# First value units on the un-normed residual, scaled afterwards, in a one-core hybrid decoder step

## What is computed

```
xn = x * rsqrt(mean(x*x) + eps) * norm_mix
lru_x, lru_g, q, k, v = split(xn @ w_in)
y_lru = (recurrence(conv(lru_x)) * gelu(lru_g)) @ w_branch_lru
q, k = rmsnorm(q, q_gain), rmsnorm(k, k_gain)         # per head
y_att = merge(three dilated window groups of q, k, v) @ w_branch_att
g_lru, g_att = sigmoid(xn @ w_merge + b_merge)
x = x + (g_lru*y_lru + g_att*y_att) @ w_o
x = x + (silu(gate) * up) @ w_ffn_out                 # gate, up = rmsnorm(x) @ w_ffn_in
```

## Time and profile before

| | us |
|---|---|
| median of 3 runs | 2105.46 |
| lowest, highest | 2101.01, 2105.50 |
| profiled execution, its own time | 2102.43 |
| its span, first to last instruction | 2100.6 |
| TensorE busy in it | 2023.8 |
| VectorE, ScalarE, GpSimd busy | 927.7, 510.1, 552.2 |

### The profile page before, as it was taken

The page is one execution under the profiler, slowest core; times in us unless marked ns, Lnnn a source line. Parts: engine busy times, 40 slices in busy tenths (PEclk is TensorE's granted clock), DMA queues, the critical chain, the costliest instruction groups (busy, mean ns, idle before and its releaser), DMA issues.

```text
span 2100.6 us, 33178 instructions
## 1 busy us (share of the span) xinstructions
PE 2023.8 (96%) x12884; PEld 1952.6 (93%) x12884; DVE 927.7 (44%) x1222; ACT 510.1 (24%) x791; POOL 552.2 (26%) x331
## 2 busy tenths in 40 slices
PE   5799999999989999999989989999999999999999
PEld 4799889999989999999988889999999999999999
DVE  8466667777714333333256563433321324202331
ACT  5466643333314433333311011210100000000000
POOL 2233322322221111111121142322323323323232
PEclk9899999999999999999999999999999999999999
DMA  3111112222252332333467353111111111111112
GB/s 128 44 43 42 42 45 80 84 96 80 90 196 86 130 126 91 126 126 112 134 229 262 121 192 140 47 45 50 41 50 50 40 50 50 40 50 46 44 53 87
DMA packets 71592, 188.39 MB, mean 90 GB/s; under 512 B 9313, under 2 KB 28796, under 8 KB 70780
## 3 DMA queue, kind: packets, MB, share of 16 engines
q1 hardware_dynamic: 41456, 136.97, 19.3%
q10 hardware_dynamic: 30092, 50.81, 6.6%
HBM read 145.09 MB, written 45.81 MB: 91 GB/s over the span
## 4 chain that ended last, share of the span: by engine, by line
PE 90%; DVE 4%; DMA 3%; issue 2%; ACT 1%; POOL 0%; SPq 0%; ACTq 0%; DVEq 0%; POOLq 0%
PE ups L485 66%; PE ups L585 13%; PE ups L610 3%; PE aux L634 3%; PE aux L509 1%; PE aux L536 1%; PE aux L622 1%; PE ups L622 1%; DMA bt_s<-u_s 1%; DVE ext L1169 1%; DMA o_s<-x 1%; DVE x L1430 0%; DMA x<-x_T 0%; DVE ext L1165 0%; DMA x<-o_s 0%
## 5 line engine op out<-in xcount | busy, mean ns | idle before, releaser
L485 PE MATMUL ups<-big,wsp 128*128 128x344 f32 x9360 | 1508.3, 322 | 18.4 <-POOL wsp L454 6.6
L485 PEld LDWEIGHTS ups<-big,wsp 128*128 128x128 f32 x9360 | 1485.7, 189 | 39.6 <-issue 26.6
L452 POOL CAST wsp<-wraw 128x1024 fp32r<-128x1024 f32 (+2 forms) x160 | 165.5, 1035 | 1494.2 <-issue 698.1
L454 POOL TENSOR_TENSOR wsp<-wraw,wsp 128x1024 fp32r<-128x1024 f32 (+2 forms) x160 | 380.7, 2380 | 12.8
L585 PE MATMUL ups<-big,wsp 128*128 128x344 f32 x1728 | 302.9, 326 | 1.6 <-ACTq L968 1.6
L585 PEld LDWEIGHTS ups<-big,wsp 128*128 128x128 f32 x1728 | 271.3, 189 | 7.1 <-issue 5.2
L1265 DVE RECIPROCAL x<-x 128x1024 f32<-128x1024 f32 x24 | 157.3, 6553 | 75.3 <-ACT x L931 75.3
L1323 DVE SCALAR_TENSOR_TENSOR x<-ups,ext 128x128 f32<-128x128 f32 (+1 forms) x192 | 58.3, 345 | 215.1 <-PE ups L610 126.2
L1128 ACT ACTIVATE ext<-ext 128x1032 f32<-128x1032 f32 x22 | 23.5, 1068 | 482.5 <-DVE ext L1529 482.4
L1531 DVE TENSOR_TENSOR ext<-ups,ext 128x1032 f32<-128x1032 f32 x22 | 27.1, 1233 | 215.4 <-PE ups L485 215.4
L1545 DVE TENSOR_TENSOR x<-ups,x 128x1032 f32 x24 | 29.6, 1233 | 203.6 <-PE ups L485 203.6
(11 more groups left out here) (187 smaller groups left out, 1114.4 us busy)
## 6 DMA issues: line engine op xcount, KB each, us to landing
...
```

Of the source, the lines that this page charges most:

```text
L452: nc.gpsimd.tensor_copy(hi, raw).then_inc(w_hi, 1)
L454: nc.gpsimd.tensor_tensor(lo, raw, hi.bitcast(F32), ALU.subtract).then_inc(w_split[slot], 1)
L485: ins = nc.tensor.matmul(ups[:, slot, c, 0:CH], wsp[:, slot, w, k, :], src[:, a, k, c * CH:(c + 1) * CH], start=(k == 0 and w + a == 0), s ...
```

## The change

The two pairs `v` move from behind the queries to the very start of `stream`. The first value pair doesn't take the normed input: ScalarE multiplies each residual tile by `norm_mix` as it lands (the high part, in `big2`), VectorE makes the low part (L1224), and TensorE multiplies it tile by tile, the second unit two tiles behind the first (`LEAD`). Squares are added by VectorE and GpSimd beside that, and the ones-products (`first_sums`) are put among the last tiles. The second value pair takes the same un-normed input. ScalarE copies the outputs (`values_out`), VectorE scales them by the reciprocal root (`values_scaled`) and then makes the normed input in place in the residual's buffers (`normed`, `normed_low`), which is first used by the first recurrence pair.

That pair runs as two whole units, with its gate products behind them. The last two gate chunks of the recurrence are put between the chunks of the first query unit. The bias lines are made before everything else. The first attention pair follows the last key unit at once, with a tile table of its own (`FIRST_PIECES`), the last head statistics inside it and the bias tile loaded behind them; query and key tiles, value tiles and others change their buffers so that they can be loaded earlier. The square sum of the decode rows goes to the stage `ylru`.

```diff
+        x_sq = big1_f32[:, 0]
+        sums, odd_sums, rinv = x_sq[:, 0, :], x_sq[:, 1, :], ext[:, 0, 0:NT]
...
+            ("v", 2, KT, A["w_in"], 40, 41, 2, 0),
             ("lru", 8, KT, A["w_in"], 0, 8, 1, 0),
             ("qk", 12, KT, A["w_in"], 16, 17, 2, 0),
-            ("v", 2, KT, A["w_in"], 40, 41, 2, 0),
...
-        QT, KTT, VT = tmp(0)[:, 0:SEQ], tmp(1)[:, 0:SEQ], tmp(2)[:, 0:SEQ]
+        QT, KTT, VT = ext[:, 2, 0:SEQ], ext[:, 3, 0:SEQ], tmp(2)[:, 0:SEQ]
...
+        FIRST_PIECES = (16, 24, 28, 31, 34, 37, 40, 42, 44, 46, 48)
...
-            for k in range(KT):
-                sp.dma_start(tmp(k), A["x_T"][k]).then_inc(x_loaded[k], 16)
...
+                if name == "v":
+                    first = 1
+                    weights(0, 0)
+                    for k in range(KT):
+                        sp.dma_start(tmp(k), A["x_T"][k]).then_inc(x_loaded[k], 16)
+                        if k == 1:
+                            weights(0, 1)
+                    for dst, con in consts:
+                        sp.dma_start(dst, con).then_inc(const_ld, 16)
...
-                        sp.wait_ge(qn_stored[j], 16 * 13)
-                        sp.wait_ge(v_stored[j], 16)
-                    sp.wait_ge(sq_normed, 1)
+                        sp.wait_ge(v_stored[j], 16 * 2)
+                    sp.wait_ge(qn_stored[0], 16 * 8)
+                    query_loads(0, 0)
+                    sp.wait_ge(qsl_done[0], 12)
                     value_load(0, 0)
                     sp.wait_ge(bt_fill, 16)
-                    query_loads(0, 0)
-                if name == "lru":
-                    first = 1
-                    weights(0, 0)
-                    weights(0, 1)
-                    for dst, con in consts:
-                        sp.dma_start(dst, con).then_inc(const_ld, 16)
+                    sp.wait_ge(st_done[1], 13)
+                    bias_load(0, 0)
...
+                    pool.wait_ge(nsq_done, 5)
+                    nc.gpsimd.tensor_tensor(odd_sums, odd_sums, x_sq[:, 4, :], ALU.add).then_inc(odd_done, 1)
+                    pool.wait_ge(nsq_done, 8)
+                    pool.wait_ge(odd_done, 1)
+                    nc.gpsimd.tensor_tensor(odd_sums, odd_sums, x_sq[:, 7, :], ALU.add).then_inc(odd_done, 1)
+                    split(name, nk, 1, 0)
+                    split(name, nk, 1, 1)
+                    low(POOL_LOW[0])
+                    continue
+                if name == "lru":
+                    first = 1
+                    split(name, nk, 0, 0)
+                    low(POOL_LOW[1])
+                    low(POOL_LOW[2])
+                    split(name, nk, 0, 1)
...
+            pe.wait_ge(lines_ld, 48)
+            bias_line(0)
+            bias_line(1).then_inc(u_ps, 1)
+            pe.wait_ge(u_sb, 1)
+            bias_line(2).then_inc(u_ps, 1)
...
+            LEAD = 2
+            for n in range(KT + LEAD):
+                if n < KT:
+                    if n == 0:
+                        pe.wait_ge(w_split[0], T0["v"] + 2)
+                        pe.wait_ge(ps_free[0], T0["v"] + 1)
+                    pe.wait_ge(xlo_done, n + 1)
+                    raw_tile(0, n)
+                if n == 7:
+                    pe.wait_ge(u_sb, 2)
+                    pe.wait_ge(ones_done, 1)
+                    pe.wait_ge(sum_done, 1)
+                    first_sums(0)
+                    first_sums(1)
+                if n == 8:
+                    pe.wait_ge(nrt_done, 1)
+                    first_sums(2)
+                if n >= LEAD:
+                    if n == LEAD:
+                        pe.wait_ge(w_split[1], T0["v"] + 2)
+                        pe.wait_ge(ps_free[1], T0["v"] + 1)
+                    raw_tile(1, n - LEAD)
+            unit("v", 1, 0, big2)
+            unit("v", 1, 1, big2)
...
+            unit("lru", 0, 0, big1, ready=normed_ready)
+            unit("lru", 0, 1, big1)
+            gates(0, 0)
+            with pe.Fori(1, KT) as i:
                 for c in range(NCH):
-                    unit("lru", i, 0, big1, parts=(c,), ready=partial(wait_split, pe, 0) if first else None)
-                    if first:
-                        unit("lru", i, 1, big1, parts=(c,))
-                    elif c < 2:
+                    unit("lru", i, 0, big1, parts=(c,))
...
-            gates(KT - 1, 1)
-            gates(KT - 1, 2)
-            pe.wait_ge(gate_ev, KT * NCH + 1)
...
+                    if first and j == 0:
+                        for c in range(2):
+                            unit("qk", i, j, big1, parts=(c,))
+                            gates(KT - 1, c + 1)
+                        pe.wait_ge(gate_ev, KT * NCH + 1)
+                    else:
+                        unit("qk", i, j, big1, parts=(0, 1))
...
-            unit("v", 0, 0, big1, parts=(0, 1))
-            stats(1, 11)
-            unit("v", 0, 0, big1, parts=(2,))
-            pe.wait_ge(rt_done[1], 13)
-            pe.wait_ge(lines_ld, 48)
-            bias_line(0)
-            bias_line(1).then_inc(u_ps, 1)
-            unit("v", 0, 1, big1)
-            pe.wait_ge(u_sb, 1)
-            bias_line(2).then_inc(u_ps, 1)
-            pe.wait_ge(sm_dve, 1)
-            nc.tensor.matmul(aux[:, 1, 0:192], bones[:], sqs, start=True, stop=True).then_inc(sm_pe, 1)
-            unit("v", 1, 0, big1)
-            unit("v", 1, 1, big1)
...
-                    if g == 0:
+                    if first:
+                        stats(1, 11)
+                        pieces(8, marks[0])
                         pe.wait_ge(ps_free[1], T0["att0"] + 1)
-                        pe.wait_ge(u_sb, 2)
-                        pe.wait_ge(sm_act, 1)
+                        pe.wait_ge(rt_done[1], 13)
...
+                if g == 0:
+                    pair(0, True, FIRST_PIECES)
+                with pe.Fori(int(g == 0), 4) as i:
+                    pair(i, False, PIECES)
...
-            y_chunks(0, 3)
+            y_chunks(0, 1)
+            head_squares()
+            y_chunks(1, 3)
...
+            act.dma_start(gmix[:], A["c_norm_mix"]).then_inc(gmix_ld, 16)
+            act.dma_start(lines.rearrange("p (g n) -> p g n", g=NG), A["c_lines"].rearrange("g b n -> b g n")).then_inc(lines_ld, 16)
+            act.dma_start(relx[0:NBK, :], A["rel_bias"]).then_inc(lines_ld, 16)
+            act.dma_start(relx[NBK:NBK + 1, :], A["c_one"]).then_inc(lines_ld, 16)
+            act.wait_ge(gmix_ld, 16)
             for k in range(KT):
-                square(0, k, k % 2)
+                act.wait_ge(x_loaded[k], 16)
+                nc.scalar.activation(big2[:, 0, k, :], tmp(k), ACT.Identity, scale=gmix[:, k:k + 1]).then_inc(xhi_done, 1)
+                nc.scalar.activation(x_sq[:, k, :], tmp(k), ACT.Square).then_inc(nsq_done, 1)
+                if k == 2:
+                    act.wait_ge(u_sb, 2)
...
+            values_out(0)
+            values_out(1)
+            values_store(0)
+            values_store(1)
+            for k in range(4):
+                normed_hi(k)
+            values_out(2)
+            for k in range(4, KT):
+                normed_hi(k)
+            values_store(2)
...
+            values_out(3)
+            values_store(3)
...
+            act.wait_ge(sm_pe, 1)
+            nc.scalar.activation(rms, aux[:, 1, 0:192], ACT.Sqrt, scale=1.0 / HD, bias=epst[:]).then_inc(sm_act, 1)
...
+            dve.wait_ge(u_ps, 1)
+            nc.vector.tensor_copy(u_lines[:, 0:2, :], aux[0:HG, :, 0:UL]).then_inc(u_sb, 1)
+            dve.wait_ge(u_ps, 2)
+            nc.vector.tensor_copy(u_lines[:, 2, :], aux[0:HG, 0, 0:UL]).then_inc(u_sb, 1)
             for k in range(KT):
-                norm_add(k, 0, k % 2)
+                dve.wait_ge(xhi_done, k + 1)
+                nc.vector.scalar_tensor_tensor(big2[:, 1, k, :], tmp(k), gmix[:, k:k + 1], big2[:, 0, k, :].bitcast(F32),
+                                               ALU.mult, ALU.subtract).then_inc(xlo_done, 1)
+                if k > 1 and k not in POOL_LOW:
+                    dve.wait_ge(nsq_done, k + 1)
+                    step.step(nc.vector.tensor_tensor(sums, sums, x_sq[:, k, :], ALU.add))
+            dve.wait_ge(odd_done, 2)
+            nc.vector.tensor_tensor(sums, sums, odd_sums, ALU.add).then_inc(sum_done, 1)
+            for c in range(NCH):
+                dve.wait_ge(nrt_done, c + 1)
+                step.step(nc.vector.reciprocal(part(rinv, c), part(rinv, c)))
+
+            def values_scaled(n):
+                j = n % 2
+                dve.wait_ge(ps_free[j], n // 2 + (T0["v"] + 2))
+                nc.vector.tensor_tensor(VO[j], VO[j], rinv, ALU.mult).then_inc(vm_done, 1)
+
+            def normed(k):
+                nc.vector.scalar_tensor_tensor(tmp(k), tmp(k), gmix[:, k:k + 1], rinv, ALU.mult, ALU.mult).then_inc(nf_done, 1)
+
+            def normed_low(k):
+                if k not in POOL_LOW:
+                    dve.wait_ge(nhi_done, k + 1)
```

(17 more changed lines are left out.)

240 lines of the change are left out of this document (101 added, 139 removed).

## The result

The changed kernel takes 2087.81 us (median of 4 runs, 2086.37 to 2091.51), the kernel before 2104.51 in the same comparison (4 runs): a ratio of 0.9923, 95% interval 0.9906 to 0.9940. A repeat on another chip gave 2085.91 (5 runs) against 2103.62, 0.9921 (0.9908 to 0.9935). Forecast was 2078 with a range of 2066 to 2090 and 0.95 on faster. Direction and range held, but by the profiled executions the gain is 16.1 us (2102.43 to 2086.37) where the sum said 25.7.

A forecast was written before the change was run, and what follows sets the result against it. TensorE was busy 2023.8 of 2100.6 us, leaving some 77 us idle and a little low clock. Terms 15.6 + 3.5 - 45.8 + 1.0 = -25.7 took 2102.43 to 2076.7, as a median 2078, range 2066 to 2090.

The forecast's parts named there:

- (a) to (c): Start up to the first value pair and sums: first low part done at 13.0 us, this stretch ending at 39.6.
- (d): Second value pair beside VectorE's norming, to 62.2 us: last low part ready about 62.5, wanted 65.5; cover 3, charged 2.
- (B): Rival: port collisions of VectorE and GpSimd in the start come out in full, about +7 us, giving 2085; chance 17%.
- the rule from the Trainium skill: VectorE instructions with two SBUF inputs contend with GpSimd instructions reading SBUF; passes take 3.24 us against 1.23.
- The mark set for (B): Profile sign at the first recurrence gates: forecast near 87 us; a start later than 92 means (B) holds.
- The end of the recurrence: Last gates moved into the first query unit: gain 0.3 us, cold restart +2.8, GpSimd's weight split +1.0; sum +3.5.
- (A): Rival: no wait at the first query statistics, since the chain behind the last gate shortens; up to -12 us, 2067; 8%.
- From the last key unit to attention: Hand-over into attention: scores start 43.5 us earlier, idle gaps of 2.7 and 4.5 us; sum -45.8.
- E: End of the last unit before attention, about 563.4 us; scores start at E + 60.4 before, E + 16.9 after.
- The decode rows: Square sum and root moved into the next stage, nearly all hidden by VectorE's idle time: 0 to 3 us, taken as 1.
- The sum: Whole kernel: 15.6 + 3.5 - 45.8 + 1.0 = -25.7 us, from the profiled 2102.43 to 2076.7.
- (C): Rival: every two-input VectorE pass of the start takes 3.24 us, about 50 us in all, giving 2128; chance 2%.

## Why the prediction was right and where it fell short

- **The start, (a) to (c).** First product 14.82 for 13.0, end of the first pair 41.73 for 39.6: 2 us late. The bias tables landed at 7.65, not at 6.0 (an estimate); the rest, 0.5, is not assigned. What the prediction calls the low clock of the first products is read from their durations (488 ns and later 319): the profile's windows give a granted clock of 1.00 there.
- **(d), the cover of the normed input.** This is the term that was mis-sized, and it is nearly the whole miss. I gave the cover as 3 us and charged 2 for collisions. The four waits are 1.40 + 1.50 + 1.60 + 2.13 = 6.6, and the products between and behind them took 4.2 us more than in a warm stream (three single tiles take 2.72 for 1.4, and the 123 take 22.30, at 0.157 each 19.4). That is 10.9 for 2; the three other executions with the same start give 10.8, 11.4 and 9.5. Behind it lies VectorE's chain: from 44.13 to 71.24, the end of the last normed tile, it needed 27.1 us for 14 passes that the prediction had at 17.4. Some 8.5 us of that are passes beside GpSimd's work. 1.85 are the wait for ScalarE behind its store issue, which the prediction had at nothing. Rival (B) named this, with its own sum of +7 for 2085, the rule from the Trainium skill, page "SBUF — State Buffer", section "Who interferes with whom", stood beside it, and the text then chose the cheaper value in spite of the earlier trace rows. The rule held in the rows shown: 3.43, 3.37 and 3.31 beside GpSimd for 1.22 to 1.24 without, and 3.56 for 0.75. What (B) itself left out is the clock: it priced the collisions, not what a row of short waits costs behind them. The prediction had seen the clock fall some 4 us into an idle stretch; here it fell to 0.50 with no wait longer than 2.13.
- **The mark set for (B).** "If the first gates start later than 92, (B) holds": they start at 97.94, and without the collisions at 87.27, where the forecast said 86.9. What the sum had of the start is right but for the collisions and what they bring with them.
- **The end of the recurrence.** +3.5 forecast, +3.2 measured (1.5 ahead of the statistics, 1.7 behind). Ahead of them the sum had +0.7 (GpSimd's split at 1.0, less the gain of 0.3), and the split cost 1.5; the restart was 1.65 (up to 2.5 in other executions) where 2.8 was said. Two errors that cancel, which is luck, but the reason (the chain behind the last gate is VectorE's and ScalarE's) is shown by the gates put back. (A) fell.
- **From the last key unit to attention.** Forecast -45.8; from the end of the last key unit to the start of `ylru` it is -45.2. The idle times are 2.69 and 3.53, forecast 2.7 and 4.5, and the low clock in the first scores is there in both. That E itself is later by the start's loss doesn't touch it.
- **The decode rows.** 1.0 forecast, -0.7 measured, from the start of `ylru` to the end. The sparse queries' second row of products starts 32.7 us behind that mark in both kernels: free, as their cover promised. The 0.7 lie between there and the feed-forward, without a cause shown.
- **The sum.** 26.6 + 3.2 - 45.2 - 0.7 = -16.1, as measured. From the second attention pair to `ylru` are 408.1 and 408.5 us, from the feed-forward's sums to the end 747.0 and 747.1: these stages didn't change their length. (C), the slower end, stayed far off: the mean pass beside GpSimd's work is long, but only some of the passes meet it.
